# A Strassen in-projection on one core: low halves of weights from a PSUM copy, products joined from PSUM, row factor on the tokens

## What is computed

```
def rmsnorm(x, g, eps=1e-6):
    return x * rsqrt(mean(x * x, axis=-1) + eps) * g

h = rmsnorm(x, attn_norm)        # x: (2304, 1024)
proj = h @ w_in                  # w_in: (1024, 4096)
q, k, v, z = split(proj, 4)      # later: attention of q, k, v, then * silu(z), @ w_out
```

## Time and profile before

| | us |
|---|---|
| median of 3 runs | 3154.04 (3152.27 to 3157.59) |
| profiled execution | 3157.8 |
| its span, first to last instruction | 3156.0 |

### The profile page before, as it was taken

One profiled execution on the slowest core, in us unless ns is written; L12 is line 12 of the kernel. 1 busy time (PEld: TensorE's weight loads), 2 busy tenths in 40 slices (PEclk: granted clock), 3 DMA queues, 4 the chain that ended last, 5 costly groups with the idle time before them and its releaser, 6 DMA issues. The chain is left out here.

```text
span 3156.0 us, 43070 instructions
## 1 busy us (share of the span) xinstructions
PE 2880.2 (91%) x15098; PEld 2519.9 (80%) x15098; DVE 2268.1 (72%) x2448; ACT 1595.6 (51%) x2838; POOL 1321.8 (42%) x758
## 2 busy tenths in 40 slices
PE   3879788978898999999999999999799899899799
PEld 3878787878896878787878787878588799897687
DVE  8999999999987878787878787878778400241332
ACT  3434443444436777776777677777444321222321
POOL 4777877788861222222222222222466221130552
PEclk7989898999998999999999999999999999999899
DMA  2455244425544441314141414112465531464753
GB/s 83 149 154 157 78 149 151 122 80 160 161 131 123 160 101 36 101 36 101 34 102 34 103 35 102 34 47 74 141 207 174 207 118 65 133 195 155 260 179 112
DMA packets 281836, 374.24 MB, mean 119 GB/s; under 512 B 22923, under 2 KB 258507, under 8 KB 276140
## 3 DMA queue, kind: packets, MB, share of 16 engines
q1 hardware_dynamic: 279404, 369.14, 38.5%
q10 hardware_dynamic: 2080, 2.10, 0.2%
q0 software_dynamic: 128, 0.13, 0.0%
HBM read 258.04 MB, written 125.97 MB: 122 GB/s over the span
## 5 line engine op out<-in xcount | busy, mean ns | idle before, releaser
L1266 DVE TENSOR_REDUCE pa_half_max<-pa_score 128x1 f32<-128x1024 f32 x512 | 625.6, 1222 | 235.5 <-PE pa_score L1054 234.6
L1357 POOL TENSOR_SCALAR pa_p<-pa_p,pa_inv_sum,pa_lam_neg 128x2048 f32<-128x2048 f32 x128 | 262.8, 2053 | 947.4 <-DVE pa_inv_sum L1293 947.4
L206 PE MATMUL ia_acc<-ia_xh,ia_wh 128*128 128x384 f32 x1344 | 475.1, 354 | 175.7 <-DVE ia_c L715 102.7
L1200 ACT ACTIVATE pa_p<-pa_score,pa_neg_max 128x1024 f32<-128x1024 f32 x512 | 568.3, 1112 | 76.0 <-DVE pa_neg_max L1272 72.8
L1113 PE MATMUL pa_o_acc<-pa_wt,pa_vv 128*128 128x256 f32 x2048 | 510.3, 380 | 1.1 <-ACT pa_o_out_s L1235 0.3
L1050 PE MATMUL pa_score<-pa_ka,pa_qa 128*128 128x512 f32 x1024 | 456.8, 446 | 21.3 <-ACT pa_p L1200 9.6
L207 PE MATMUL ia_acc<-ia_xl,ia_wh 128*128 128x384 f32 x1344 | 468.2, 348 | 0.0
L208 PE MATMUL ia_acc<-ia_xh,ia_wl 128*128 128x384 f32 x1344 | 467.3, 348 | 0.0
L1180 ACT ACTIVATE pa_wt<-pa_turned 128x512 f32<-128x512 f32 x512 | 306.4, 599 | 261.4 <-PE pa_turned L1082 260.8
L1054 PE MATMUL pa_score<-pa_kb,pa_qb 96*128 96x512 f32 x1024 | 424.3, 414 | 0.0
L442 POOL TENSOR_TENSOR ia_w_sums<-ia_raw 128x512 f32<-128x512 f32 x240 | 384.4, 1605 | 86.2 <-PE ia_acc L208 53.5
(11 more groups left out here) (280 smaller groups left out, 5123.9 us busy)
## 6 DMA issues: line engine op xcount, KB each, us to landing
ia_raw<-attn_w_in SPq DMA_DIRECT2D x46, 1024.0 KB, 7.0
qk_hi<-ia_hi SPq DMA_DIRECT2D x96, 192.0 KB, 4.3
qk_lo<-ia_c SPq DMA_DIRECT2D x96, 192.0 KB, 3.5
pa_ka<-qk_hi SPq DMA_DIRECT2D x32, 512.0 KB, 6.5
fl_slices<-normed SPq DMA_DIRECT2D x26, 512.0 KB, 6.5
ia_h<-x_cols SPq DMA_DIRECT2D x24, 384.0 KB, 5.7
v<-ia_c SPq DMA_DIRECT2D x48, 192.0 KB, 5.3
attn_gate<-ia_c SPq DMA_DIRECT2D x48, 192.0 KB, 2.0
```

What stands on the lines that cost most here:

```text
L206: pe.matmul(out, a_hi(k), b_hi(k), start=first and n == 0, stop=False)
L1200: act.activation(dst[:, half * HALF:(half + 1) * HALF], score[:, (4 * q + j) % RING].rearrange("p a b -> p (a b)"), ACT.Exp, bias=neg_max[ ...
L1266: dve.tensor_reduce(half_max[:, q % 2, n, half:half + 1], score[:, (4 * q + j) % RING].rearrange("p a b -> p (a b)"), AX_X, ALU.max).then_ ...
```

## The change

*Low halves.* The banks of the products are 6 instead of 8. The last two hold full-precision copies of the weight operand: after `wh` of a set, ACT writes the same source to bank 6 or 7 in turn (semaphore `w_up`), as soon as the low half of two sets before is done; `weight_low` subtracts `wh` from that copy.

*Joins.* ACT takes only three products, M2 to C21, M1 to C22, M3 to C12. DVE makes 8 joins a quad (`fuse`), each with one product read from its bank: C21 += M4 in slot t = 2; C11 = C22 + M4 and C22 -= M2 in t = 4; C12 += M5, C11 -= M5, C22 += M3 in t = 5; C11 += M7 in t = 6; C22 += M6 in t = 0 of the next quad. POOL's joins are gone.

*Row factor.* In span 0 POOL multiplies all four tiles by it. In spans 1 and 2 `weigh` multiplies the tokens by the norm weight and the row factor in one instruction, and no tile is scaled. (The words "two of three pairs" in the change's name are these two spans.) Squares and loads of the next span's tokens come one quad earlier (j = 1 to 8), roots and inverses at j = 9 instead of 11, `weigh` at j = 10 to 13 instead of 2 to 9.

*Token sums.* Three sums are made in place by DVE (`x_ready_sum`, in spans 1 and 2 at j = 14) and two by POOL from them.

The diff, in the order constants, POOL, PE, ACT, DVE:

```
-    BANKS = 8
+    BANKS = 6
+    FUSED = 8
...
+        def w_scratch(s):
+            return acc[:, BANKS + s % 2]
...
+        DONE = (1, 4, 7, 8)
+        def wait_tile(eng, n, k):
+            if n < W_PAIRS:
+                eng.wait_ge(scaled, 4 * n + k + 1)
+            else:
+                eng.wait_ge(fused, FUSED * n + DONE[k])
...
                 def x_add(p, i):
+                    wait(pool, products, SETS * W_PAIRS * p - SETS + i + 1)
+                    pool.wait_ge(x_ready, 3 * p + 3)
+                    pool.tensor_tensor(x_sums[:, i], first_sum(p), x_source(p, 1 if i == 5 else 3), ALU.add).then_inc(x_sum, 1)
+                def scale(n, k):
+                    if n < W_PAIRS:
+                        half = 1 if k in (C12, C22) else 0
+                        pool.wait_ge(inverted, half + 1)
+                        pool.wait_ge(fused, FUSED * n + DONE[k])
+                        pool.tensor_tensor(tile(n, k), tile(n, k), rstd[:, 0, half], ALU.mult).then_inc(scaled, 1)
...
+                    if slot in (0, 1):
+                        x_add(0, slot + 5)
+                    if 0 < span < SPANS and ahead_set in (5, 6):
+                        x_add(span, ahead_set)
...
+                            scale(n, C21)
+                        if t == 6:
+                            scale(n, C12)
+                            low(n, C21)
+                    if n and t == 0:
+                        scale(n - 1, C11)
+                    if n and t == 1:
+                        scale(n - 1, C22)
+                    if n and t == 2:
+                        low(n - 1, C11)
...
-                    elif i in (M4, M1):
-                        pe.wait_ge(copies_out, 4 * q + i + 1)
+                    elif i == M1:
+                        pe.wait_ge(copies_out, 3 * q + 2)
                     else:
-                        pe.wait_ge(fused, 6 * q + {M2: 1, M5: 3, M3: 4, M7: 5, M6: 6}[i])
+                        pe.wait_ge(fused, FUSED * q + {M2: 3, M4: 2, M5: 5, M3: 6, M7: 7, M6: 8}[i])
...
                     act.activation(wh[:, s % RING], src, ACT.Copy).then_inc(w_hi, 1)
+                    wait(act, w_lo, s - 1)
+                    act.activation(w_scratch(s).rearrange("p (k n) -> p k n", n=P), src, ACT.Copy).then_inc(w_up, 1)
...
-                            take(n, t - 1, (C21, C11, C22, C12)[t - 1])
+                        if t == 1:
+                            take(n, M2, C21)
+                        if t == 3:
+                            take(n, M1, C22)
+                        if t == 4:
+                            take(n, M3, C12)
...
-                        finish(n, C12)
...
+                    if n and t in (0, 1, 2):
+                        finish(n - 1, (C12, C11, C22)[t])
...
+                        if p:
+                            x = dve.scalar_tensor_tensor(out=h[:, k, half], in0=h[:, k, half], scalar=norm_w[:, k:k + 1],
+                                                         in1=rstd[:, p % 2, half], op0=ALU.mult, op1=ALU.mult)
...
-                    src = w_sums[:, s % RING] if i in SUMMED else w_terms(n, i)[0]
-                    dve.tensor_tensor(wl[:, s % RING], src, f32(wh[:, s % RING]), ALU.subtract).then_inc(w_lo, 1)
+                    dve.wait_ge(w_up, s + 1)
+                    dve.tensor_tensor(wl[:, s % RING], w_scratch(s).rearrange("p (k n) -> p k n", n=P), f32(wh[:, s % RING]),
+                                      ALU.subtract).then_inc(w_lo, 1)
...
+                def fuse(n, no):
+                    c21, c12, c11, c22 = (tile(n, k) for k in range(4))
+                    out, x, i, op = ((c21, c21, M4, ALU.add), (c11, c22, M4, ALU.add), (c22, c22, M2, ALU.subtract),
+                                     (c12, c12, M5, ALU.add), (c11, c11, M5, ALU.subtract), (c22, c22, M3, ALU.add),
+                                     (c11, c11, M7, ALU.add), (c22, c22, M6, ALU.add))[no]
+                    dve.wait_ge(products, SETS * n + i + 1)
+                    dve.wait_ge(copies_out, 3 * n + (1, 2, 2, 3, 3, 3, 3, 3)[no])
...
+                    dve.tensor_tensor(out, x, bank(n, i), op).then_inc(fused, 1)
...
+                        for no in {2: (0,), 4: (1, 2), 5: (3, 4, 5), 6: (6,)}.get(t, ()):
+                            fuse(n, no)
+                        if n == 0 and t in (5, 6):
+                            invert(0, t - 5)
                     if n and t == 0:
+                        fuse(n - 1, 7)
...
+                        if j == 9 and t in (3, 6):
+                            invert(p + 1, t // 6)
+                        if 10 <= j < 14 and t in (2, 6):
+                            weigh(p + 1, 2 * (j - 10) + t // 6)
+                        if j == 14 and t in (1, 3, 5):
+                            x_ready_sum(p + 1, t // 2)
```

More of the change, by code:

```diff
@@ L332, in x_part, with first_sum, x_source @@
             return h[:, HALF_K * j:HALF_K * j + HALF_K, half]
[L334 to L337, removed]
+        def first_sum(p):
+            return f32(hi[:, 1]) if p == 0 else squares[:].rearrange("p a b t -> p (a b) t")
+        def x_source(p, i):
+            return (x_part(0, 0), x_part(1, 0), first_sum(p), x_part(0, 1), x_part(1, 1), x_sums[:, 5], x_sums[:, 6])[i]
+        READY = (0, 1, 2, 3, 0)
         def sums_upto(s):
             return len(SUMMED) * (s // SETS) + sum(i in SUMMED for i in range(s % SETS + 1))
[L343 to L350, removed]
+        def w_scratch(s):
+            return acc[:, BANKS + s % 2]
         def unit_at(p, e):
@@ L454, in x_add, with low @@
                 def x_add(p, i):
[L455 to L458, removed]
+                    wait(pool, products, SETS * W_PAIRS * p - SETS + i + 1)
[7 more added lines that the diff above has]
+                        pool.tensor_tensor(tile(n, k), tile(n, k), rstd[:, 0, half], ALU.mult).then_inc(scaled, 1)
+                def low(n, k):
+                    if kind_of(n) == "split":
+                        pool.wait_ge(out_hi, acts_before(n) + k + 1)
+                        pool.tensor_tensor(tile(n, k).bitcast(F32R), tile(n, k), f32(tile_hi(n, k)), ALU.subtract).then_inc(out_lo_pool, 1)
                 weight_sum(0)
@@ L476, in _ @@
                     p, j = divmod(n, W_PAIRS)
+                    span = p if j < 8 else p + 1
+                    ahead_set = slot - SETS * W_PAIRS * span + 6
+                    if slot in (0, 1):
+                        x_add(0, slot + 5)
+                    if 0 < span < SPANS and ahead_set in (5, 6):
+                        x_add(span, ahead_set)
                     if n < QUADS:
                         if t == 3:
-                            pool.wait_ge(copies_out, 4 * n + 2)
-                            pool.tensor_tensor(tile(n, C21), tile(n, C21), tile(n, C11), ALU.add).then_inc(joined, 1)
@@ L481, in _ @@
[L481 to L487, removed]
```

146 lines of the change are left out of this document (47 added, 99 removed).

## The result

| | before | after |
|---|---|---|
| median, us | 3153.15 (4 runs, 3148.79 to 3157.59) | 3025.47 (4 runs, 3021.63 to 3030.89) |
| profiled execution, us | 3157.8 | 3030.89 |
| its span, us | 3156.0 | 3029.0 |

A forecast was written before the change was run, and what follows sets the result against it. DVE bounds the in-projection; once relieved, PE does. Of 221.6 us above PE's floor 75 stay, saving 147: the profiled 3157.8 becomes 3011, and with the median 3.8 lower, 3008 us; range 2985 to 3058.

The forecast's parts named there:

- The bound and the floor: In-projection: DVE bounds it; PE's floor is 14.56 us a quad, 698.9 for 48; the products took 221.6 more.
- The weight subtraction: DVE's weight low halves (L659): 0.68 us each with one PSUM input, 336 times, 228 us in place of 449.
- The copies on ACT: ACT's 336 new copies of 512 elements to PSUM: bounds 0.48 and 0.64, taken as 0.6 us each, 202 us.
- six banks are too few: Rival, PE's product banks: ordinary quads keep stalling 2.6 us each, 113 us come back, 3121 us; chance 0.08.
- the token loads come one quad earlier, into work that has ended: Step on SP's queue: store and load order stays, next span's token loads move a quad earlier; no cost counted.
- Squares: Excess at j = 9: inverse ahead of the join freeing M2's bank, ring two places shorter; 2 x 3 = 6 us.
- Changes of span and quad 0: Excess that stays: 2 x 10 = 20 us around span changes, from token subtractions and clock loss; 34 in quad 0.
- POOL in quads 1 to 8: Excess there: 7 us once from POOL's first scaling waiting for the inverse, plus 8 x 0.8 = 6.
- The signs: Trace marks expected: subtraction 0.68, copies near 0.6, later quads 14.56, quads 1 to 8 15 to 16, DVE 80 to 85%.
- POOL in DVE's place: Rival: POOL keeps its medians, quads 1 to 8 cost 18.2 us each, 28 us more, 3036 us; chance 0.13.
- DVE not relieved: Rival: the 512-element subtraction stays near 1.3 us beside POOL, 45 us more over 24 split quads, 3053; chance 0.06.
- alternation: Rival: ACT's copy and DVE's subtraction take turns through two scratch banks, 24.2 us a quad, +241, 3395; chance 0.05.

The follow-up runs named there:

- the last experiment: The kernel before, with only the next span's token loads issued one quad earlier (j = 1 to 8 instead of 2 to 9): 3136.56 us, ratio 0.9942.

## Why the prediction was right, and where it was off

*The bound and the floor* were right: DVE at 96% was what held PE, and with DVE relieved PE runs at 14.56 us a quad in 32 of 48 quads.

*The weight subtraction* was forecast at 0.68 us and 228 us in sum; 0.684 and 227.7 were measured (the instructions overlap a little, so the sum is below 336 x 0.684). The row that decided it was L715 in the earlier trace rows, an instruction of another line with one input in PSUM and a flat duration. The Trainium skill, "VectorE: DVE Perf Modes", section "The TRN2 errata — SBUF-src ops pay a fixed extra latency per instruction", lists 62 cycles more for a PSUM source than for one in SBUF, an estimate of 65 ns at its 0.96 GHz. The trace doesn't agree for this two-input subtraction: the shortest took 627 ns with PSUM and 622 without (raw weights; 672 for sums), and the median with PSUM was 685.

*The copies on ACT*: 0.6 forecast, 0.590 measured, against 0.627 for ACT's rounding of the same source into SBUF (to fp32r, but the format seems not to count: 384 elements from SBUF to SBUF took 0.515 us to fp32r and 0.517 to fp32). The Trainium skill, "ScalarE: Activation LUTs", section "Step-by-step: what each stage is for", calls PSUM the faster destination, and the trace agrees by 37 ns. Its proviso, that TensorE must not need most of PSUM, was the rival "six banks are too few". It did not come about: from quad 33 on there is no stall, and even five banks cost only 13 us on the kernel with early loads.

*Other rows*: DVE's lows took 0.918 us instead of the 1.50 that I carried over, presumably because POOL was less often beside them. POOL's weight sums took 1.402 in the mean and 1.300 in the median where I had 1.29, and its scalings 1.195. The token scaling took 0.986 (0.606 to 1.380) between bounds of 0.54 and 1.50; none of the 32 reached the upper one.

*The step that failed* is the one that cost the token loads at nothing: "the token loads come one quad earlier, into work that has ended". The squares that read them moved by the same quad, so ACT went on waiting for them. In the kernel before ACT waited for these loads as follows (the first span's share is 3.2 us), and one wait out of quad 5 beside its load:

```profile
ACT ia_square L547 <- DMA ia_h<-x_cols: 86.8, 13, 7.3
...
ACT ia_squares L547 <- DMA ia_h<-x_cols: 28.7, 4, 8.7
```

```profile
148.42 0.47 SPq L374 DMA_DIRECT2D ia_h<-x_cols  x1
...
154.17 0.85 ACT L547 ACTIVATE ia_square<-ia_h 128x768 f32<-128x768 f32 x1 [7.32 <-DMA ia_h<-x_cols]
```

ACT stood there from 146.85, before SP had even issued the load, and so it was with all 16 loads of the next spans: ACT came up to 3.3 us before the issue and waited 5.3 to 8.7 us, 112 in sum. After the change it comes 2.0 to 3.6 us behind the issue and waits 0.6 to 5.6 us, 44 in sum. So the change did not make the loads later for ACT, and the wait even got shorter; but with DVE relieved, what queued behind it reached PE. I had read it as the harmless wait of an engine that isn't the bound. Loads a quad earlier are worth 27.5 us in the new kernel and, by the last experiment, 17 in the old. With the loads out of the way the excess is 68.3 us, below my 75.

*Squares*: the term of quads 9 and 25 was sized at 6 us and measured 17.6. Its mechanism (an inverse ahead of the joins) was there: removed alone it gave back 7.0 us in these quads. The larger part was the same late load: early loads alone gave back 13.6, both edits together 15.0.

*Changes of span and quad 0*: 20 forecast, 18.2 measured; 34 and 38.7. *POOL in quads 1 to 8*: 13 and 15.4, but of another make than I said, and that the two are so near is luck: in quads 2 to 8 about 10 of it were the late loads and the squares behind them. Without them 6.4 remain, nearly all in quad 1, where I had counted 7; the 6 for ordinary quads came to nothing, with POOL at 14.5 us of 14.56.

*The signs.* Of those that the prediction named, the subtraction's 0.68 without spread, the copies near 0.6 and quads 33 to 47 at 14.56 came. The last product ended at 812.7 and not near 791, and quads 1 to 8 took 14.6 to 19.2 us, 16.5 in the mean, not 15 to 16. Quads 21, 23, 24 and 25 took 16.3 to 24.2 us, above the 15.5 from which the prediction called its count on PE alone wrong for the later spans. PE's releaser there was DVE's join, and behind it stood ACT with the late load (in quad 25 the inverse too), not too few banks: with the same 6 banks and early loads the first three stand at 14.56. DVE was busy 70% of the stage (572.9 of 813 us), not 80 to 85, which is the split quads' 12.1 of 14.56 taken for all quads, with the lows at 1.50.

*Slips in the sums*, none above 2 us: the third span's first quad is 23.4 over the floor, not 24.2; 32 scalings at 1.50 in place of 0.54 are 31 us, not 29; and 3011 less 3.8 is 3007.

*The rivals.* POOL in DVE's place: the time was 3025, between forecast and this rival's 3036, but quads 3 to 8 at 14.56 with early loads exclude it. DVE not relieved falls with the subtraction at 0.684, too few banks with quads 33 to 47 at 14.56, alternation with the run on one scratch bank.

## What to carry to other kernels

When the engine that sets the end is relieved, go through the waits of all other engines again, each with what is queued behind it: a wait that looks hidden in the old bound can be the next one's cause (here 17 us of the old time, 27.5 of the new), and it may be a transfer with several queues between it and the engine that stalls. For fp32 subtractions beside a busy POOL, look at whether both inputs lie in SBUF; one input in PSUM took DVE out of POOL's way even though ACT had to write a copy for it. And price a part of a change both ways, first in and last out: the copy with its two banks was worth 75 and 31 us.

## What was unexpected of the hardware

Busy time of an engine isn't its work: in the kernel before, an edit that touched only when DMAs were issued took 14 us off DVE's busy time (895 to 881) with the same instructions. And the disturbance between DVE and POOL is mutual. POOL's weight sum in the kernel before, and its shortest, median and longest in the change (before: 1258, 1609 and 2821 ns in the earlier trace rows):

```profile
L442 POOL TENSOR_TENSOR ia_w_sums<-ia_raw 128x512 f32<-128x512 f32 x240 | 384.4, 1605 | 86.2 <-PE ia_acc L208 53.5 <-DMA ia_raw<-attn_w_in 32.7
```

```profile
L443 POOL TENSOR_TENSOR ia_w_sums<-ia_raw x240: 1259/1300/2822, 8.9 to 792.2; 128x512 f32<-128x512 f32 x120
```

The mean is 1.605 us beside DVE's two-SBUF-input work, 1.525 with fewer such instructions (the copy undone, 6 banks), and 1.402 with the weight subtraction out of SBUF.
